# A two-block layer in one core: a bias brought in by transfer, and other addresses for weights and activations

## The reference

```
mod = c @ w_ada + b_ada                      # 1024 -> 6 x 1024, once per block
shift, scale, gate, shift2, scale2, gate2 = split(mod, 6)
h = norm(x) * (1 + scale) + shift            # second block: x*(1+sc)+sh
proj = h @ w_in                              # 4872 columns; second block 2848
...
x = x + gate * rms_norm(mix, g_post_mix)     # second: layer_norm(ALPHA*x + gt1*mix)
h = norm(x) * (1 + scale2) + shift2
f = (silu(h @ w_gate) * (h @ w_up)) @ w_down # width 2816
x = x + gate2 * rms_norm(f, g_post_ffn)
```

## Time and profile before

| | |
|---|---|
| median of three runs | 850.78 us (850.25 to 852.6) |
| profiled execution: its time | 851.24 us |
| its span, first to last instruction | 849.4 us |
| PE busy | 805.3 us, 95% |
| DVE busy | 641.1 us, 75% |
| ACT busy | 389.7 us, 46% |
| chain by engine | PE 76%, DVE 16%, ACT 3%, issue 2%, DMA 2% |
| products L2284 to L2286 with whi, ffh, ffl | 3 x 168 |
| mean granted clock of TensorE | 0.985 |

### The profile page before, as it was taken

The page is one execution under the profiler, slowest core; times in us unless marked ns, Lnnn a source line. Parts: engine busy times, 40 slices in busy tenths (PEclk is TensorE's granted clock), DMA queues, the critical chain, the costliest instruction groups (busy, mean ns, idle before and its releaser), DMA issues.

```text
span 849.4 us, 16656 instructions
## 1 busy us (share of the span) xinstructions
PE 805.3 (95%) x7026; PEld 736.3 (87%) x7026; DVE 641.1 (75%) x845; ACT 389.7 (46%) x543; POOL 12.6 (1%) x32
## 2 busy tenths in 40 slices
PE   2999999999899999999998999989998999999996
PEld 2898898999579999998877987889877999999874
DVE  5879788888978786867778899887388767555456
ACT  3366843944364444443345875411125544444340
POOL 0100000000000000000001000000000000000000
PEclk9999999979899999999999999999999999999998
DMA  9994656653858888977983644700053679565531
GB/s 361 333 315 144 194 186 214 229 192 124 265 169 286 296 284 280 335 266 258 386 273 98 222 125 147 216 12 4 28 179 116 202 239 331 154 191 177 198 100 49
DMA packets 95832, 173.71 MB, mean 205 GB/s; under 512 B 7575, under 2 KB 55038, under 8 KB 95758
## 3 DMA queue, kind: packets, MB, share of 16 engines
q1 hardware_dynamic: 92784, 165.86, 58.6%
q0 software_dynamic: 1744, 5.84, 2.1%
q10 hardware_dynamic: 1230, 0.95, 0.4%
HBM read 171.58 MB, written 1.05 MB: 203 GB/s over the span
## 4 chain that ended last, share of the span: by engine, by line
PE 76%; DVE 16%; ACT 3%; issue 2%; DMA 2%; DVEq 0%; SPq 0%; ACTq 0%
PE bank L2021 14%; PE bank L2023 13%; PE bank L2022 13%; PE bank L2284 4%; PE bank L2286 4%; PE bank L2285 4%; PE bank L2455 3%; DVE acc L448 3%; DVE wlo L427 2%; PE bank L1996 2%; PE bank L1998 2%; PE bank L1997 2%; PE bank L1952 1%; DMA raw<-in_w_in 1%; DVE arena L448 1%
## 5 line engine op out<-in xcount | busy, mean ns | idle before, releaser
L573 ACT ACTIVATE whi<-raw 128x1024 fp32r<-128x1024 f32 (+2 forms) x216 | 224.7, 1051 | 262.3 <-PE bank L2023 118.9
L427 DVE TENSOR_TENSOR wlo<-raw,whi 128x1024 fp32r<-128x1024 f32 (+2 forms) x216 | 259.0, 1214 | 99.8 <-ACT whi L573 96.1
L2021 PE MATMUL bank<-hh,whi 128*128 128x256 f32 x1016 | 287.1, 283 | 3.3 <-DVE hl L1094 2.9
L2023 PE MATMUL bank<-hh,wlo 128*128 128x256 f32 x1016 | 285.2, 281 | 0.0
L2022 PE MATMUL bank<-hl,whi 128*128 128x256 f32 x1016 | 285.1, 281 | 0.0
L2021 PEld LDWEIGHTS bank<-hh,whi 128*128 128x128 f32 x1016 | 192.3, 189 | 6.4 <-issue 5.6
L2023 PEld LDWEIGHTS bank<-hh,wlo 128*128 128x128 f32 x1016 | 191.5, 189 | 0.0
L2022 PEld LDWEIGHTS bank<-hl,whi 128*128 128x128 f32 x1016 | 191.4, 188 | 0.0
L448 DVE SCALAR_TENSOR_TENSOR acc<-raw,cc,acc 128x1024 f32<-128x1024 f32 x77 | 98.6, 1280 | 7.7 <-DMA raw<-in_w_ada 3.4
L2284 PE MATMUL bank<-whi,ffh 128*128 128x512 f32 x168 | 66.5, 396 | 0.8 <-DVE wlo L427 0.8
L2285 PE MATMUL bank<-wlo,ffh 128*128 128x512 f32 x168 | 66.1, 393 | 0.0
(11 more groups left out here) (439 smaller groups left out, 1050.4 us busy)
## 6 DMA issues: line engine op xcount, KB each, us to landing
raw<-in_w_ada SPq DMA_DIRECT2D x96, 512.0 KB, 5.0
raw<-in_w_in SPq DMA_DIRECT2D x54, 512.0 KB, 4.6
raw<-in_w_ffn_in SPq DMA_DIRECT2D x88, 256.0 KB, 3.8
raw<-in_w_ffn_gate SPq DMA_DIRECT2D x44, 256.0 KB, 4.4
raw<-in_w_ffn_up SPq DMA_DIRECT2D x44, 256.0 KB, 5.3
raw<-in_w_ffn_down SPq DMA_DIRECT2D x22, 512.0 KB, 5.6
raw<-in_w_ffn_out SPq DMA_DIRECT2D x22, 512.0 KB, 3.3
raw<-in_w_out SPq DMA_DIRECT2D x16, 512.0 KB, 5.0
```

Of the source, the lines that this page charges most:

```text
L427: eng.tensor_tensor(lo[:, 0:nk * width], raw[:, b % RAW, 0:nk * width], hi[:, 0:nk * width].bitcast(fp), ALU.subtract)\
L573: act.activation(weight_place(g)[0][:, 0:nk * width], raw[:, b % RAW, 0:nk * width], ACT.Copy)\
L2021: mm(o, wh[:, k, c], xh[:, kk_, :], start=first, stop=False)
L2023: last = mm(o, wl[:, k, c], xh[:, kk_, :], start=False, stop=end)
```

## The change

It does three things.

1. Addresses. ARENA grows by 32 numbers and SLOT shrinks to 1024. A helper `pad` puts filler before arena and before whi, so that these start at multiples of 256. Modulo 256 bytes the tensors then start at: arena (with ffh, ffl, mgh, mgl) 0, hh and hl 192, raw 192 in all its six places, whi and wlo 0 in all four places. HL stays 4 and RAW stays 6.
2. Since two rows of 520 columns don't fit into 1024 numbers, o_if is cut into eight blocks of one row instead of four blocks of two; the slices of `split` and `prepare` are adapted, and the wait on h_ready counts rows.
3. The gates' bias. GpSimd zeroes all of acc and brings 1024 biases into its first partition, once `piece_done` d is there; VectorE's first step of a gate part waits for that DMA (`spreads` at 16 x BIAS_AT[d]) and adds to acc instead of overwriting it. TensorE's products with bmod go.

```diff
-SLOT = 2 * 520
+SLOT = 1024
+BIAS_AT = {4: 8, 5: 11, 10: 12, 11: 17}
...
+        def pad(to):
+            n = (to - -(-nc.sbuf_base // 32) * 32) % 256 // 4
+            if n:
+                sb(f"pad{to}_{nc.sbuf_base}", [P, n])
-        ARENA = 20496
+        ARENA = 20528
+        pad(0)
...
         raw = sb("raw", [P, RAW, SLOT])
+        pad(0)
...
-                nk = 4 if name == "kva" else 2
+                nk = {"kva": 4, "o_if": 1}.get(name, 2)
...
-                    eng.tensor_scalar(to, x, by, None, ALU.mult).then_inc(sem(f"{me}_blocks"), 1)
+                    if d in GATES:
+                        eng.wait_ge(sem("spreads"), 16 * BIAS_AT[d])
+                        ins = eng.scalar_tensor_tensor(to, x, by, to, ALU.mult, ALU.add)
+                    else:
+                        ins = eng.tensor_scalar(to, x, by, None, ALU.mult)
+                    ins.then_inc(sem(f"{me}_blocks"), 1)
...
+            def gate_bias(d):
+                i, c0 = PARTS[d]
+                pool.wait_ge(sem("piece_done"), d)
+                pool.memset(acc[:, :], 0.0).then_inc(sem("pads"), 1)
+                pool.wait_ge(sem("pads"), 8 + GATES.index(d))
+                pool.wait_ge(sem("spreads"), 16 * (BIAS_AT[d] - 1))
+                pool.dma_start(acc[0:1, :], A[("b_ada", "b_ada_2")[i]][0:1, c0:c0 + D]).then_inc(sem("spreads"), 16)
...
-                        mm(bank[at + h][:, :], C("ones"), acc[:, 512 * h:512 * h + 512], start=True, stop=False)
-                        for t in range(4):
-                            x = c0 // P + 4 * h + t
-                            last = mm(bank[at + h][:, t * P:(t + 1) * P], bmod[:, i, x:x + 1].to_broadcast([P, P]),
-                                      ident, start=False, stop=t == 3)
+                        last = mm(bank[at + h][:, :], C("ones"), acc[:, 512 * h:512 * h + 512], start=True, stop=True)
...
-                        pe.wait_ge(sem("h_ready"), half_ready + i + 1)
+                        pe.wait_ge(sem("h_ready"), half_ready + nk * i // 2 + 1)
```

More of the change, by code:

```diff
@@ L491, in _ @@
             spread(bc[:, 1, :], A["g_post_ffn"][0], sem("spreads"))
+            gate_bias(4)
             pool.wait_ge(sem("h_ready"), 8)
@@ L494, in _ @@
             spread(bc[:, 3, :], A["emb_ln_b_2"], sem("spreads"))
+            gate_bias(5)
+            gate_bias(10)
             pool.wait_ge(sem("xhat_ready"), 2)
@@ L512, in _ @@
             spread(bc[:, 3, :], A["ln2_b_2"][0], sem("spreads"))
+            gate_bias(11)
         def flat(name):
@@ L612, in _ @@
                    .then_inc(sem("xn_ready"), 1)
-            split("o_if", slice(0, 2))
+            split("o_if", slice(0, 4))
             scale_h(0)
-            split("o_if", slice(2, 4))
+            split("o_if", slice(4, 8))
             act.dma_start(cst[:, 258:CONST_N], A["const"][:, 258:CONST_N]).then_inc(sem("const_in"), 16)
@@ L1108, in _ @@
             prepare("c3")
-            prepare("o_if", slice(0, 1))
+            prepare("o_if", slice(0, 2))
             g_pre = v1T[:, v1["g_pre_mix"][0]:v1["g_pre_mix"][1]]
@@ L1119, in _ @@
             scale_h(0, second_half)
-            prepare("o_if", slice(1, 2))
             prepare("o_if", slice(2, 4))
+            prepare("o_if", slice(4, 8))
             prepare("qm")
@@ L1603, in _ @@
             prepare("r", slice(0, 1))
-            dve.wait_ge(sem("spreads"), 9 * 16)
+            dve.wait_ge(sem("spreads"), 10 * 16)
             ln_affine(2, bc[:, 2, :], bc[:, 3, :])
@@ L1878, in _ @@
             prepare("gf0", slice(3, 4))
-            dve.wait_ge(sem("spreads"), 13 * 16)
+            dve.wait_ge(sem("spreads"), 16 * 16)
             ln_affine(3, bc[:, 0, :], bc[:, 1, :])
@@ L1935, in part @@
                 if d in GATES:
-                    i, c0 = PARTS[d]
                     for h in range(2):
-                        mm(bank[at + h][:, :], C("ones"), acc[:, 512 * h:512 * h + 512], start=True, stop=False)
-                        for t in range(4):
-                            x = c0 // P + 4 * h + t
-                            last = mm(bank[at + h][:, t * P:(t + 1) * P], bmod[:, i, x:x + 1].to_broadcast([P, P]),
-                                      ident, start=False, stop=t == 3)
+                        last = mm(bank[at + h][:, :], C("ones"), acc[:, 512 * h:512 * h + 512], start=True, stop=True)
                 elif d == 1:
```

## The result

The changed kernel took 843.59 us (median, 842.68 to 845.71), the kernel before beside it 851.41 us (850.25 to 852.6): a ratio of 0.9909, 95% interval 0.9887 to 0.9931. So it is faster by 7.8 us, more than the 0.3% that can be told from nothing; the forecast was 840.2. The profiled execution took 843.57 us with a span of 841.8, against 851.24 and 849.4.

A forecast was written before the change was run, and what follows sets the result against it. Bound: TensorE's 3240 products of 256 columns, 89% on the chain. Terms -10.8 - 1.6 - 6.8 + 1.5 + 4.7 + 2.4 = -10.6 us, from a median of 850.78 to 840.2 us; 8 in 10 for 833 to 851.

The forecast's parts named there:

- 256-column products, at full clock: TensorE's products with hh or hl: 113 ns apart in all ring places at distance 64; -10.8 us, bounds -14.2 and +4.9.
- 512-column products: TensorE's products with ffh and wo at distance 0, 227 ns for ffh, with h-by-weights rows; -1.6 us, between 0 and -3.
- four gate parts: Gate parts around 231, 289, 627 and 719 us lose their 128-column products with bmod; -6.8 us.
- piece 5 late: Gate piece beside ff: bias lands at 267.6 us, VectorE stands 6.9 us, TensorE loses time; +1.5 us, 0.5 to 4.
- piece 10: Gate piece whose accumulator is free 5.8 us ahead: its bias lands just in time; 0.
- start, hold: Before qm: ScalarE's small DMAs wait behind o_if copies, so qm starts at 52.2, not 47.50; +4.7 us, 3.5 to 6.
- start, clock: Behind the idle gap before qm TensorE gets a lower clock; half of 4.8 us taken: +2.4 us, 0 to 3.3.
- Which one is it after?: 256-column products at distance 64: of two steady spacings, 113 and 118 ns, it took 113.
- the 1.8 us that I took off for VectorE: 256-column gain cut by 1.8 us because VectorE, preparing blocks beside a piece of w_ada, has little time to spare.
- Rival A: 256-column products get no faster, distance 64 stays in its 118 ns rhythm; 850.3 us, chance 0.17.
- Rival B: Start costs nothing: DMAs issue another way or the 5 us are found again behind 107 us; 833.1 us, chance 0.12.
- rival C: All 256-column products lock at 119.6 ns because the weights' absolute address decides; 855.9 us, chance 0.06.

The follow-up runs named there:

- e_w64: Changed kernel with weights moved to 64 and h to 0 modulo 256 bytes, so their distance stays 64; 843.88 us.
- e_h0: Changed kernel with h alone moved 64 bytes further, to 0 modulo 256 bytes, so the distance to the weights is 0; 854.13 us.
- e_addr_o4: Kernel before with the new addresses alone: o_if still in four blocks, bias still by products with bmod; 841.64 us.
- e_p5: Changed kernel with GpSimd fetching part 5's bias ahead of the two emb_ln broadcasts; 840.18 us.
- e_addr_only: Changed kernel without the bias change: new addresses and o_if in eight half blocks; 847.33 us.
- e_start: Changed kernel with 17 of ScalarE's 18 small DMAs ahead of its first o_if copy, the 672 KB one between copies four and five; 840.25 us.
- e_bias_only: Kernel before with only the gates' bias by transfer; addresses, ring places and o_if's four blocks as before; 848.4 us.
- e_o4p5: Changed kernel with o_if back in its old four blocks of two rows and part 5's bias fetched first; 834.68 us.

## Why the prediction was right, point by point

The kernel is faster by more than can be told from nothing, and 843.59 lies in the range of 833 to 851; the forecast of 840.2 was 3.4 us too low. By terms, from the starts in the two traces:

| term | predicted | measured |
|---|---|---|
| 256-column products, at full clock | -10.8 | -8.7 |
| 512-column products | -1.6 | -2.5 |
| four gate parts | -6.8 | -6.6 (-7.6, and +1.0 in the product behind three of them) |
| piece 5 late | +1.5 | +2.5 |
| piece 10 | 0 | +0.5 |
| start, hold | +4.7 | +4.5 |
| start, clock | +2.4 | +2.6 |
| sum | -10.6 | -7.7; the spans differ by 7.6 |

**Part 1** was right in its mechanism: the distance and not the address (e_w64, e_h0), all places alike, and a gain of the forecast's kind, confirmed alone at 9.9 us (e_addr_o4). One step of it failed: "Which one is it after?" I concluded from the neighbours in the earlier trace rows that the 118 ns rhythm was handed on by a place at another distance, and from two restarts in the earlier trace rows that distance 64 starts at 113. Distance 64 has both rhythms of its own: in the changed kernel all four places have it, and 51 blocks still run at 117.6. That the two restarts read were both at 113 was chance; 8 of 25 after were not. The 51 blocks at 117.6 ns are 51 x 24 x 4.4 ns = 5.4 us of products; the 1.8 us that I took off for VectorE covered a part of them by accident, since VectorE cost nothing there (e_addr_o4). Rival A and the forecast are the two ends of what really is a mixture, and the number fell between them, as the range had allowed. By the Trainium skill, "TensorE: Matmul & The Clock Gate", section "Step-by-step: what each phase is for", loading the next weights takes no read bandwidth from the running product. Read as the prediction read it, that addresses can't matter, the measurement is against it once more: 120 ns at distance 0 and 113.3 at 64 for the same instruction, 854.13 and 843.59 us. Why the distance matters no run shows.

The 512-column products reached 227 ns (2.72 us for 12) in every place of the ring, as forecast, in 36 of the 44 blocks with ffh (the others took 228 to 233), here in dA:

```profile
405.68 0.39 PE L2309 MATMUL bank<-whi,ffh 128*128 128x512 f32 x1
408.40 0.39 PE L2309 MATMUL bank<-whi,ffh 128*128 128x512 f32 x1
...
413.84 0.39 PE L2309 MATMUL bank<-whi,ffh 128*128 128x512 f32 x1
```

The mean before was taken too low (230; most blocks of dA took 229, 234, 233 and 228 ns in turn), so the term came out at the far end of its bounds.

**Part 2.** Gate parts: right in size, by two errors of opposite sign. Three of them are shorter by 2.1 us, not 1.7, but the second product behind each of these now comes 0.32 us later, and part 10 gains only 1.3, since VectorE's hl ends behind it at 627.4 and TensorE waits for that. Piece 5: the time of the bias was right to the tenth (267.6 plus the shift of 2.5 is 270.1), VectorE's standing too (6.9 against 6.77); what was missed is the second stop, one item on. It was called "what VectorE loses further it partly wins back"; it won back nothing until the gate part. e_p5 shows that both stops hang on this one wait. Piece 10: the bias was in time, as forecast. The 0.46 us came from the memset, which the prediction counted as hidden: VectorE's small step, a TENSOR_SCALAR, ends with it. By the Trainium skill, "SBUF — State Buffer", section "SBUF: two separate sides", GpSimd shares a pair of ports with those steps of VectorE that run in a mode with two ports, or that have two inputs while GpSimd reads too, and whoever holds the pair holds it to the end of its instruction. The trace agrees, with 424.88 against 424.85 us, and with the two-input steps beside memsets, which only write, at their usual 1.22 us; which mode the small step ran in no trace shows. The rule could have been applied ahead, since the memset stood in the change.

**Part 3.** Hold and clock were within 0.3 us, and the signs came at their places (the DMA row from 40.96, the copy at 49.63, 0.50 behind it). For the clock that is partly luck: the "half of 4.8 us" rests on no row, and no run shows it; measured are 2.6 us, mostly one block at 213 ns per product. For the hold the reason was one of two. Undone alone, the DMAs give back 3.3 us in the medians, and 4.9 of 7.0 in the profile; what is left goes with a block of half the size taking a whole place in raw, too. The prediction counted the places of whi and wlo (four) and not those of raw (six), and read no GB/s. Its number was right because the two causes overlap and the later one, ScalarE's queue, was the one priced: the copy began at 49.63 in the changed kernel, and with the DMAs out of the way the transfer held it until 46.68. Rival B (the start costs nothing) is refuted by e_addr_only against e_addr_o4, 5.7 us; rival C (119.6 ns everywhere, by the absolute address of the weights) is refuted: with the weights at 0 the changed kernel runs at 113 and 118 ns and e_h0 at 120, which is what distance 0 gives.

A small slip of reading, without weight in the sum: 2.84 us for 24 products are 118.3 ns, not 118.5.

## What to carry to other kernels

Where TensorE is dense with products whose weights are loaded anew each time, lay out weights and moving operand by their distance modulo 256 bytes and measure it at a few distances: of those seen here 64 bytes was best for 256 columns with the weights standing still (up to 6% per product against distance 0), and 0 for 512 columns with the weights moving. When a layout forces smaller blocks, count the places of every ring that the blocks pass through, the transfers' ring too: a half block takes a whole place in each, and what stands behind it in each queue waits. When a stop is explained by one releaser, take it away and see which comes next before its whole length is booked as a gain: e_start brought 3.3 us of the 7.1 forecast, and qm started at 49.05; with the four blocks back it started at 47.35.

## What the runs showed of the hardware that was not expected

- Two rhythms of the same stream of products at the same addresses, 113.2 and 117.6 ns at a distance of 64 bytes and 117.3 and 118.7 at 96, set at a restart and kept until the next.
- The rate depends on the distance in steps finer than 64 bytes, without order: 120, 118.3, 113.3 or 117.8, 117.3 or 118.7, 118.5, 117.8 ns at 0, 32, 64, 96, 128 and 192 bytes.
- An eight-column TENSOR_SCALAR of VectorE took 0.80 instead of 0.17 us beside a memset of GpSimd, in the traces of the changed kernel, e_bias_only (0.80) and e_o4p5 (0.81) alike; a TENSOR_TENSOR of 1024 columns beside the same memsets took no longer than elsewhere.
- The clock falls in some traces and not in others at one place: from 506.8 to 513.8 us e_addr_o4's products run at about half the rate (0.43 us from start to start for 512 columns, instead of 0.23), and at the same place of its program the changed kernel was granted 1.00. TensorE's work there came 3.1 us later for it.

```profile
506.00:516.00 10.00, 10.00 (x29) 6.79 (x28) 9.61 (x14) 2.97 (x4) 0.00 (x0) 0.66 0.48 151
```

This is from e_addr_o4's windows. So the profiles of two such kernels can differ by some 3 us for the clock and some 4 for the rhythm, and differences of that size were read here from starts at the same place, not from the totals.
